# Building the expert gates with one-hots in bf16, tokens innermost, and a VectorE product in place of GpSimd's

## What is computed

```python
def peer_ffn(x, w_peer_q, peer_subkeys, peer_u, peer_v):
    ...
    top_s, top_i = lax.top_k(s, PEER_TOPK)
    ...
    i1 = jnp.take_along_axis(top_i[..., 0, :], best_c // PEER_TOPK, axis=-1)
    i2 = jnp.take_along_axis(top_i[..., 1, :], best_c % PEER_TOPK, axis=-1)
    experts = i1 * N_KEYS + i2
    gates = jax.nn.softmax(best_s, axis=-1).astype(x.dtype)
    ...
        u = peer_u[ec]
        act = jax.nn.gelu(jnp.einsum('tkd,td->tk', u, xc))
        return jnp.einsum('tk,tkd->td', gc * act, peer_v[ec])
```

## Time and profile before

| what | value |
|---|---|
| time of the runs, median of 3 | 4363.92 us (4361.32 to 4364.85) |
| span of the profiled execution, first to last instruction | 4368.1 us, 78341 instructions |
| TensorE's mean granted clock in it | 0.927 |
| busy: TensorE / its weight loads / VectorE / ScalarE / GpSimd | 90% / 85% / 41% / 37% / 71% |
| moved by DMA | 713.80 MB, mean 163 GB/s |

### The profile page before, as it was taken

How to read it: one execution, slowest core, us unless ns; L and a number is a source line. 1 busy time by engine, 2 the same in 40 slices (tenths; PEclk the granted TensorE clock), 3 DMA queues, 4 the chain that set the end, 5 groups by cost and what they waited for, 6 DMA issues and landing times.

```text
span 4368.1 us, 78341 instructions
## 1 busy us (share of the span) xinstructions
PE 3910.7 (90%) x31206; PEld 3717.4 (85%) x31206; DVE 1792.1 (41%) x2279; ACT 1609.7 (37%) x2267; POOL 3110.1 (71%) x1292
## 2 busy tenths in 40 slices
PE   9699996878998899989998999957999999399987
PEld 1599995878987888979998999947999999399986
DVE  0667357844023244263024294175443000944433
ACT  0212432233323333354443344454444444544442
POOL 0357960856755664868888798878887888788864
PEclk9799997989978999999999999968999999599998
DMA  9366740733433442535544455513554555045532
GB/s 348 120 241 262 268 184 1 283 129 137 173 115 109 142 151 88 186 132 188 188 164 154 178 180 182 185 45 125 182 185 173 190 182 185 7 164 182 186 143 97
DMA packets 98368, 713.80 MB, mean 163 GB/s; under 512 B 11040, under 2 KB 11168, under 8 KB 12064
## 3 DMA queue, kind: packets, MB, share of 16 engines
q1 hardware_dynamic: 97344, 705.75, 44.6%
q10 hardware_dynamic: 864, 5.76, 0.3%
HBM read 709.37 MB, written 2.10 MB: 163 GB/s over the span
## 4 chain that ended last, share of the span: by engine, by line
PE 71%; DVE 15%; issue 6%; POOL 5%; ACT 2%; DMA 1%; DVEq 1%; POOLq 0%; ACTq 0%; SPq 0%
PE bank L473 48%; PE bank L841 17%; POOL unit_lo L420 5%; PE bank L534 2%; DVE hot L1854 1%; DMA ring<-in_w 1%; DVE peer_w L1868 1%; PE bank L520 1%; DVE log_a L1745 1%; DVE hot L1861 1%; DVE ada_acc L1167 1%; DVE rms_tmp L1610 1%; PE bank L626 1%; DVE v1f L1577 1%; PE bank L608 1%
## 5 line engine op out<-in xcount | busy, mean ns | idle before, releaser
L420 POOL TENSOR_TENSOR unit_lo<-ring,unit_hi 128x1024 fp32r<-128x1024 f32 x1140 | 2870.9, 2534 | 871.9 <-ACT unit_hi L865 871.0
L473 PE MATMUL bank<-xl_hi,unit_hi 128*128 128x256 f32 x5696 | 1616.2, 284 | 152.1 <-POOL unit_lo L420 57.0
L865 ACT ACTIVATE unit_hi<-ring 128x1024 fp32r<-128x1024 f32 x1140 | 1175.0, 1056 | 1384.1 <-PE bank L473 589.7
L473 PE MATMUL bank<-xl_lo,unit_hi 128*128 128x256 f32 x5696 | 1605.6, 282 | 0.0
L473 PE MATMUL bank<-xl_hi,unit_lo 128*128 128x256 f32 x5696 | 1604.9, 282 | 0.0
L473 PEld LDWEIGHTS bank<-xl_hi,unit_hi 128*128 128x128 f32 x5696 | 1085.8, 191 | 166.9 <-issue 68.9
L473 PEld LDWEIGHTS bank<-xl_lo,unit_hi 128*128 128x128 f32 x5696 | 1085.7, 191 | 0.1
L473 PEld LDWEIGHTS bank<-xl_hi,unit_lo 128*128 128x128 f32 x5696 | 1085.1, 191 | 0.0
L841 PE MATMUL bank<-w_r,unit_hi 128*128 128x256 f32 x4096 | 727.8, 280 | 6.9 <-DVE w_r L1892 6.9
L841 PEld LDWEIGHTS bank<-w_r,unit_hi 128*128 128x128 f32 x4096 | 628.7, 189 | 7.1 <-issue 7.1
L841 PE MATMUL bank<-w_r,unit_lo 128*128 128x256 f32 x2048 | 574.1, 280 | 0.0
(11 more groups left out here) (363 smaller groups left out, 4371.9 us busy)
## 6 DMA issues: line engine op xcount, KB each, us to landing
ring<-in_w SPq DMA_DIRECT2D x671, 1024.0 KB, 4.8
resid<-in_xT ACTq DMA_DIRECT2D x1, 2048.0 KB, 12.7
tmp_ctx<-in_ctxT ACTq DMA_DIRECT2D x1, 2048.0 KB, 10.7
out<-resid SPq DMA_DIRECT2D x4, 512.0 KB, 2.6
con<-in_con ACTq DMA_DIRECT2D x1, 576.0 KB, 3.3
con<-in_con ACTq DMA_DIRECT2D x1, 448.0 KB, 6.2
p_tmp<-in_pT ACTq DMA_DIRECT2D x1, 256.0 KB, 3.3
vec<-in_vec ACTq DMA_DIRECT2D x1, 246.0 KB, 4.5
```

The costliest lines, as they stand in the source:

```text
L420: pool.tensor_tensor(lb[b][:], ring[slot][:, f * HALF:(f + 1) * HALF], hb[b][:].bitcast(F32), ALU.subtract).then_inc(lo_done, 1)
L473: mm = pe.matmul(bank[(s.t0 + tile[m]) % TILES][:, 0:T], w[b][:, (i % 8) * P:(i % 8 + 1) * P], mv[x][:, k, :], start=(k == 0 and w is hb a ...
L865: act.activation(hb[b][:], ring[slot][:, f * HALF:(f + 1) * HALF], ACT.Copy).then_inc(hi_done, 1)
```

## The change

The three one-hot tensors are laid out with the 8 tokens innermost ([P, 128, 8] in place of [P, 8, 128]). Two new tensors are filled once: `places`, the iota row in bf16, each value repeated 8 times, and `picked`, i1 and i2 in bf16. The comparisons read these two, so that all their operands are bf16. GpSimd's two products are taken out; VectorE makes both in one instruction, `hot_parts`, behind `hot_1`, ahead of the loop and in its body. ScalarE's activations and TensorE's matmuls read and write the new layout, in which the elements of one token lie 8 elements (16 bytes) apart.

```diff
-        oa = [zone("hot1_0", 96, [P, TG, NKEY], BF16), zone("hot1_1", 98, [P, TG, NKEY], BF16)]
-        oe = [zone("hot2_0", 100, [P, TG, I2], BF16), zone("hot2_1", 101, [P, TG, I2], BF16)]
-        ob = [zone("hotg_0", 102, [P, 3, TG, I2], BF16), zone("hotg_1", 105, [P, 3, TG, I2], BF16)]
+        oa = [zone("hot1_0", 96, [P, NKEY, TG], BF16), zone("hot1_1", 98, [P, NKEY, TG], BF16)]
+        oe = [zone("hot2_0", 100, [P, I2, TG], BF16), zone("hot2_1", 101, [P, I2, TG], BF16)]
+        ob = [zone("hotg_0", 102, [P, 3, I2, TG], BF16), zone("hotg_1", 105, [P, 3, I2, TG], BF16)]
+        places = nc.alloc_sbuf_tensor_at("places", [P, NKEY, TG], BF16, offset=z0 + 116 * KB)
+        picked = nc.alloc_sbuf_tensor_at("picked", [P, 2, T], BF16, offset=z0 + 112 * KB)
...
-                    if s.name in ("peer_u0", "peer_u1"):
-
-                        pool.wait_ge(S("gate_parts"), 1)
-                        with pool.Fori(0, T // TG // 2) as it:
-                            for k in range(2):
-                                before = int(s.name[-1]) * (T // TG) + k + 1
-                                pool.wait_ge(S("hot_2"), before + it * 2)
-                                pool.wait_ge(S("g_done"), before + it * 2)
-                                for x in (1, 2):
-                                    ins = pool.tensor_tensor(
-                                        ob[k][:, x], oe[k][:], gb[:, x, bass.ds(it * (2 * TG) + k * TG, TG)].unsqueeze(2)
-                                        .to_broadcast([P, TG, I2]), ALU.mult)
-                                ins.then_inc(S("hot_g12"), 1)
...
-                                mm = pe.matmul(bank[5 + k][:, t * I2:(t + 1) * I2], oa[k][:, t, :], ob[k][:, x, t, :],
+                                mm = pe.matmul(bank[5 + k][:, t * I2:(t + 1) * I2], oa[k][:, :, t], ob[k][:, x, :, t],
...
-                            ins = act.activation(ob[k][:, 0, t, :], oe[k][:, t, :], ACT.Copy,
+                            ins = act.activation(ob[k][:, 0, :, t], oe[k][:, :, t], ACT.Copy,
...
+            go(dve.tensor_copy(picked[:], gT[:, 0:2, :]))
+            go(dve.tensor_copy(places[:], C("iota").unsqueeze(2).to_broadcast([P, NKEY, TG])))
             event("gate_parts")
...
-                    dve.tensor_tensor(oe[k][:], bc(C("iota", r * I2, (r + 1) * I2), TG),
-                                      gT[:, 1, bass.ds(i * TG, TG)].unsqueeze(2).to_broadcast([P, TG, I2]),
-                                      ALU.is_equal).then_inc(S("hot_2"), 1)
+                    dve.tensor_tensor(oe[k][:], places[:, r * I2:(r + 1) * I2, :],
+                                      bc(picked[:, 1, bass.ds(i * TG, TG)], I2), ALU.is_equal).then_inc(S("hot_2"), 1)
...
-                    dve.tensor_tensor(oa[k][:], bc(C("iota"), TG), gT[:, 0, bass.ds(i * TG, TG)].unsqueeze(2)
-                                      .to_broadcast([P, TG, NKEY]), ALU.is_equal).then_inc(S("hot_1"), 1)
+                    dve.tensor_tensor(oa[k][:], places[:], bc(picked[:, 0, bass.ds(i * TG, TG)], NKEY), ALU.is_equal
+                                      ).then_inc(S("hot_1"), 1)
+
+                def hot_parts(i, k, r=r):
+
+                    dve.wait_ge(S("hot_2"), r * groups + 1 + i)
+                    dve.tensor_tensor(ob[k][:, 1:3], oe[k][:].unsqueeze(1).to_broadcast([P, 2, I2, TG]),
+                                      gb[:, 1:3, bass.ds(i * TG, TG)].unsqueeze(2).to_broadcast([P, 2, I2, TG]), ALU.mult
+                                      ).then_inc(S("hot_g12"), 1)
...
                     hot_1(k, k)
+                    hot_parts(k, k)
...
                         hot_1(i + 2, k)
+                        hot_parts(i + 2, k)
```

## The result

| | before | after |
|---|---|---|
| median of the runs | 4362.62 us (4359.56 to 4364.85, 4 runs) | 4325.01 us (4322.62 to 4328.81, 4 runs) |
| ratio | | 0.9916, 95% interval 0.99 to 0.9932 |
| span of the profiled execution | 4368.1 us | 4327.0 us |

The account below looks back on a forecast made before the run. VectorE was taken to bound the two gate builds; 60 periods shortened from 3.74 to 2.25 us give 89.4 us, plus 2.2 makes 91.6, so 4363.9 becomes 4272 us. The range was 4254 to 4350.

Parts of the forecast that it names:

- What bounds the kernel: In the two gate builds, 121 us each, VectorE runs without a gap at 3.74 us per group of 8 tokens.
- (a): GpSimd's products leave the build; its work gives nothing, but VectorE's comparisons return to 0.69 and 1.22 us.
- (c): VectorE's new 1024-wide bf16 product in the build takes 0.69 us, 1.22 at full price; TensorE waits for it.
- (b): VectorE's bf16 comparisons, tokens innermost, take half the time per column: 0.43 and 0.69 us.
- full rate: Rival: VectorE's bf16 instructions keep full time per column; 3.49 us a group, 17 us saved, 4347; chance 0.15.
- The 0.08 us that I added for register arithmetic: On VectorE's queue, register arithmetic shows once per group, raising 2.17 us to 2.25.
- (d): Behind VectorE in the build, ScalarE's 1.94 us a group is the floor; TensorE's 1.44 also stays below 2.25.
- (e): ScalarE and TensorE operands stepped by 16 bytes cost nothing; TensorE's slowdown is hidden up to 1.56 times.
- From the period to the time: Over both builds, 60 x (3.74 - 2.25) = 89.4 us, plus 2.2, makes 91.6 us saved.
- (f): Set-up before the first build, at most 14 us, costs nothing, hidden behind 66 us of cover.
- (g): Hand-over after each build: GpSimd splits during the build, so the first w_r subtraction saves 1.1 us, twice.
- the one on stepped reads: Rival: TensorE's matmuls in the build take twice as long, 2.88 us a group, 54 us saved, 4310; chance 0.20.

Follow-up runs that it names:

- old_parts: Kernel before the change, with GpSimd's two products made by VectorE in one instruction, old layout and f32 comparisons kept; ratio 0.9948 to before.
- all_plain: Changed kernel with TensorE's two operands and ScalarE's input and output read and written contiguously, gates made from other tokens' numbers; 4264.1 us.
- b2s: Changed kernel with the 8 tokens in blocks of 2, a step of 2 elements (4 bytes), product in two instructions; 4266.9 us, 0.9785 of before.
- w_plain: Changed kernel with TensorE's weights read as contiguous runs, moving operand still at a step of 8, gates from other tokens' numbers; 4323.7 us.

## Why the prediction was right and wrong

- *What bounds the kernel*: right. VectorE set 3.74 us a group; taking GpSimd's products out shortened it (old_parts).
- *(a) and (c), GpSimd out, the product on VectorE*: right. 3.75 us a group became 3.47 by this alone (old_parts).
- *(b), the halved slope*: right, 0.42 and 0.68 us for 0.43 and 0.69. The trace of the changed kernel agrees with what the prediction cited from the Trainium skill ("VectorE: DVE Perf Modes", "The perf-mode tier table"): a two-input bf16 operation in SBUF runs at twice the f32 rate. (The four times for one-input operations is counted on that page from the plain rate; it gives them two times in f32 already.) The doubled rate does not come in every layout: old_parts' product, 16-bit throughout, took 1.21 us. The rival "full rate" is out for the changed kernel. The group's 2.17 us was right as well: all_plain has 2.14. The 0.08 us that I added for register arithmetic do not show; it stays hidden with short instructions.
- *(d), what comes next*: the pace of ScalarE, 1.94 us, holds for contiguous operands and nearly so for a step of 2 (b2s: eight in 2.04 us from the first start to the last end, 0.24 apart), not for the step of 8 that the change makes.
- *(e), the stepped operands*: **this step failed.** The text took nothing for TensorE up to 1.56 times its pace, and called a large price a rival with 0.20. The runs put in its place: 0.127 us a matmul for 0.052, 2.4 times; the moving operand alone makes it 0.116 (w_plain). TensorE so became the bound at 3.05 us a group, where the text had VectorE at 2.25. "I put nothing on ScalarE" was also wrong: 0.30 us for 0.24, 2.40 us a group. The terms, from the measured periods: 3.75 before, 3.47 with GpSimd out, 2.14 with the new types and layout if its steps were free, 2.40 with ScalarE's step, 3.05 with TensorE's. Of 1.61 us that the change makes possible, 0.91 are given back.
- *From the period to the time*: the sum counted 30 periods a build. VectorE's first two groups are made ahead, so when it is the bound they are free; when TensorE is, all 32 count: 32 x 3.05 = 98 us, with 2.8 us ahead of it and 2.2 behind makes 103, as measured. Before, 30 x 3.74 and 8.5 us made 120.7. Twice the difference is 35.4 us of the 37.6. The forecast's own upper edge was slightly off too: 2.4 us a group gives 4281 by the sum, not 4283, and 4254 belongs to 1.94 us and not to 2.0.
- *(f), set-up*: right. VectorE's contended instructions there took up to 2.90 us and ended near 2791, and TensorE stayed full, 17.00 of 17.00 us from 2775 to 2792. The cover that the text gave as 66 us is 56 by its own times (2808 to 2864); nothing hung on it.
- *(g), hand-over*: the number was right, the reason not quite. TensorE's wait for the first `w_r` is 2.28 us in place of the 3.42 of the earlier trace rows, because the subtraction meets no split. But GpSimd makes none during the build: it stood idle for 103.03 us, waiting for ScalarE's next rounding, and began again just behind the subtraction:

```profile
2959.32 0.42 DVE L1891 TENSOR_TENSOR w_r<-peer_w,w_r 128x256 fp32r<-128x256 f32 x1 [0.88 <-ACT w_r L1095]
...
2960.00 0.77 PE L830 MATMUL bank<-w_r,unit_hi 128*128 128x256 f32 x2 [2.28 <-DVE w_r L1891]
2960.20 2.38 POOL L422 TENSOR_TENSOR unit_lo<-ring,unit_hi 128x1024 fp32r<-128x1024 f32 x1 [103.03 <-ACT unit_hi L854]
```

- *The rivals*: the one on stepped reads had the mechanism. Its price, twice the matmul (2.88 us a group, 4310), was somewhat low. The rule that it named speaks of two hits on each 16-byte line (the Trainium skill, "Advanced Engine Details and Errata", "Memory Cachelines"); the runs agree with it for the moving operand: 4 bytes 1.44 us for 24 matmuls, 8 bytes 1.65, 16 bytes about 3, 32 bytes no more. The weights, stepped by 16 bytes alone, cost far less: 1.64 in place of 1.44. Where I chose wrongly was in the weight of this rival: the edit's step was certain, no row spoke against its price, and the evidence for "nothing" was only that there was room to hide 1.56 times. An unknown that no row bounded from above deserved more than 0.20.

## What to carry to other kernels

A layout is read by more than one engine: when tokens go innermost to give VectorE its halved slope, look at what the same tensor becomes for TensorE's moving operand. A step of 2 or 4 elements of bf16 gave VectorE the halved slope as well and cost TensorE little or nothing, where a step of 8 gave back over half of it. When an engine's pace is to be compared with another's, count starts, not the length of a burst, and ask how many items of the loop the new bound has to pass, including those that the old one had made ahead.

## What the runs showed of the hardware that was not expected

TensorE's price for a stepped moving operand does not follow its clock. At the very start of a build the granted clock is still 1.00, and then it falls to 0.50. In the second build of the changed kernel matmuls start (2.01 - 0.30) / 14 = 0.122 us apart ahead of the fall and (2.97 - 0.30) / 22 = 0.121 behind it:

```profile
3691.59 2.01 PE L807 MATMUL bank<-hotg,hot 128*128 128x64 bf16 x15 [3.12 <-issue]
3693.30 2.97 PE L807 MATMUL bank<-hotg,hot 128*128 128x64 bf16 x23
...
3691.60:3693.40 1.80, 1.80 (x15) 1.80 (x16) 0.42 (x1) 1.80 (x8) 0.00 (x0) 1.00 0.93 391
3693.60:3696.00 2.40, 2.40 (x23) 2.40 (x21) 1.14 (x2) 1.41 (x6) 0.00 (x0) 0.50 0.02 7
...
2880.00:2950.00 70.00, 69.27 (x552) 65.34 (x551) 50.71 (x93) 62.37 (x185) 0.00 (x0) 0.50 0.00 0
```

(Both operands are stepped in these rows.) Contiguous ones do follow it: 24 in 0.86 us at the higher level and 1.44 at the lower. The granted clock around the first is this row of the kernel before:

```profile
3715.00:3719.00 4.00, 1.48 (x30) 1.18 (x28) 0.69 (x1) 3.35 (x14) 0.00 (x0) 1.00 0.00 0
```

The prediction's hope that a slow TensorE would get the higher clock and so be saved was wrong twice: the clock would not have helped, and it was not granted. From 2880 to 2950 TensorE was busy for 69.27 of 70 us and the granted clock stayed at 0.50, the 1.2 GHz level, all the while; in the stage of f32 products behind it the clock was at 1.00. So a TensorE that the profile shows busy did not get the higher level here; why not was not tried.
